# Two-layer encoder trunk on one core: how the last two heads' outputs, the reload of the other mixture chunks and the first W_out products are ordered

## What is computed

```python
attn = latent_attention(q_nope, q_rope, k_nope, k_rope, v)      # 8 heads, 64 wide
conv = gate_b * short_conv(gate_c * conv_in, w_conv[i])         # 512 channels
mix = jnp.concatenate([group_rms_norm(attn, g_attn_out[i], N_HEADS),
                       group_rms_norm(conv, g_conv_out[i], CONV_GROUPS)], axis=-1)
x = x + rms_norm(mix @ w_out[i], g_post_mix[i])
```

## Time and profile before

| what | value |
|---|---|
| time, median of 3 runs | 2876.78 us (2875.25 to 2877.29) |
| time of the profiled execution | 2878.98 us |
| its span, first to last instruction | 2877.2 us |
| mean granted TensorE clock | 0.992 of full |
| busy: TensorE, weight load, VectorE, ScalarE | 97%, 80%, 60%, 42% |
| end of attention in layer 0 and layer 1 | about 515 to 562 us, 1927 to 1973 us |

### The profile page before, as it was taken

How to read it: one execution, slowest core, us unless ns; L and a number is a source line. 1 busy time by engine, 2 the same in 40 slices (tenths; PEclk the granted TensorE clock), 3 DMA queues, 4 the chain that set the end, 5 groups by cost and what they waited for, 6 DMA issues and landing times.

```text
span 2877.2 us, 34913 instructions
## 1 busy us (share of the span) xinstructions
PE 2799.8 (97%) x13184; PEld 2311.0 (80%) x13184; DVE 1717.7 (60%) x2300; ACT 1203.0 (42%) x1917; POOL 113.9 (4%) x105
## 2 busy tenths in 40 slices
PE   6999999899999999999999999998999999999996
PEld 5878888688888888888887788887888888888885
DVE  4367888356544444458765588872844444444786
ACT  4336777454211211226643377773621121121473
POOL 0221000000000000000012200000000000000000
PEclk9999999999999999999999999999999999999998
DMA  4121110621111111112332111134211111111232
GB/s 149 59 74 47 32 32 23 221 91 59 51 38 57 44 44 58 44 66 96 103 108 73 56 38 32 27 106 163 82 54 40 58 44 44 58 44 44 73 103 73
DMA packets 64587, 194.93 MB, mean 68 GB/s; under 512 B 8288, under 2 KB 8288, under 8 KB 64480
## 3 DMA queue, kind: packets, MB, share of 16 engines
q1 hardware_dynamic: 64480, 193.49, 20.1%
HBM read 168.22 MB, written 25.23 MB: 67 GB/s over the span
## 4 chain that ended last, share of the span: by engine, by line
PE 93%; ACT 2%; DVE 2%; DMA 1%; issue 1%; SPq 0%; ACTq 0%; DVEq 0%
PE ps L821 28%; PE ps L823 28%; PE ps L822 28%; PE ps L988 3%; PE ps L1013 2%; PE ps L1012 2%; PE ps L1022 1%; DMA mix_lo<-yl 1%; PE ps L867 0%; PE ps L889 0%; PE ps L860 0%; ACT pth L1246 0%; DMA raw<-w_units 0%; ACT pr L1426 0%; ACT hh L1246 0%
## 5 line engine op out<-in xcount | busy, mean ns | idle before, releaser
L821 PE MATMUL ps<-hh,wh 128*128 128x512 f32 x2192 | 872.1, 398 | 25.1 <-DVE wl L1633 23.8
L823 PE MATMUL ps<-hh,wl 128*128 128x512 f32 x2192 | 856.0, 391 | 0.0
L822 PE MATMUL ps<-hl,wh 128*128 128x512 f32 x2192 | 855.9, 390 | 0.0
L821 PEld LDWEIGHTS ps<-hh,wh 128*128 128x128 f32 x2192 | 413.6, 189 | 119.7 <-issue 28.4
L822 PEld LDWEIGHTS ps<-hl,wh 128*128 128x128 f32 x2192 | 413.5, 189 | 93.5 <-issue 8.7
L823 PEld LDWEIGHTS ps<-hh,wl 128*128 128x128 f32 x2192 | 413.0, 188 | 86.7
L1246 ACT ACTIVATE wh<-raw 128x1024 fp32r<-128x1024 f32 x244 | 254.7, 1055 | 390.3 <-PE ps L823 369.8
L821 PE MATMUL ps<-gh,wh 128*128 128x512 f32 x1024 | 398.6, 389 | 0.0
L823 PE MATMUL ps<-gh,wl 128*128 128x512 f32 x1024 | 398.4, 389 | 0.0
L822 PE MATMUL ps<-gl,wh 128*128 128x512 f32 x1024 | 398.3, 389 | 0.0
L1976 DVE TENSOR_TENSOR xf<-xf,ps 128x512 f32<-128x512 f32 x464 | 310.9, 684 | 146.0 <-PE ps L823 145.5
(11 more groups left out here) (137 smaller groups left out, 3028.9 us busy)
## 6 DMA issues: line engine op xcount, KB each, us to landing
raw<-w_units SPq DMA_DIRECT2D x240, 512.0 KB, 3.3
hh<-mix_hi SPq DMA_DIRECT2D x16, 512.0 KB, 6.6
hl<-mix_lo SPq DMA_DIRECT2D x16, 512.0 KB, 7.3
stage<-w_head SPq DMA_DIRECT2D x16, 320.0 KB, 2.9
xf<-x_in SPq DMA_DIRECT2D x4, 1024.0 KB, 8.9
mix_hi<-cyh SPq DMA_DIRECT2D x8, 512.0 KB, 2.6
mix_lo<-cyl SPq DMA_DIRECT2D x8, 512.0 KB, 3.7
sq<-sums SPq DMA_DIRECT2D x32, 128.0 KB, 2.8
```

The lines of the kernel that those rows point to most:

```text
L821: nc.tensor.matmul(dst, ah, bh, start=start, stop=False)
L822: nc.tensor.matmul(dst, ah, bl, start=False, stop=False)
L823: return nc.tensor.matmul(dst, al, bh, start=False, stop=stop)
```

## The change

Heads 6 and 7 write the high and low part of their normalised output directly into chunk 3 of `hh`/`hl` (`high_at`, `low_at`); their stores to DRAM and the reload of chunk 3 are gone. Chunks 4, 7, 0, 1, 2 are loaded in SyncE's block of head 6 instead of head 7. The splits of W_out's units 0 to 3 are spread: unit 0 in head 6, units 1, 2, 3 in head 7. On TensorE, parts of outputs 0 and 1 stand between the last head's steps, and `var.1` of head 7 between the parts of output 2. The diff, cut to what the steps need:

```diff
-MIX_STORED = 16 * 2 * (CONV // P + 2 * HEADS)
+MIX_STORED = 16 * 2 * (CONV // P + 2 * (HEADS - 2))
...
 ATT_PE = steps("""
...
-q.1.0 turn.0.4.1 pv.0.1.0 pv.0.1.1 score.0.7 turn.0.5.0 turn.0.5.1 q.1.1 turn.0.6.0 turn.0.6.1 score.1.0
-pv.0.2.0 turn.0.7.0 turn.0.7.1 var.0.0 score.1.1 pv.0.2.1
+q.1.0 turn.0.4.1 pv.0.1.0 pv.0.1.1 score.0.7 turn.0.5.0 turn.0.5.1 mix.0.0 q.1.1 turn.0.6.0 turn.0.6.1 mix.0.1
+score.1.0 pv.0.2.0 turn.0.7.0 turn.0.7.1 var.0.0 mix.1.0 score.1.1 pv.0.2.1
...
 ATT_ACT = steps("""
-high.0.0.0 high.0.0.1 exp.0.1 y.-1.0 k.1.0 v.1.0 exp.0.2 high.0.1.0 high.0.1.1 exp.0.3 k.1.1 v.1.1 out.-1.1
-high.0.2.0 high.0.2.1 square.-1.1 high.0.3.0 high.0.3.1 unit.0 ln.-1.1 exp.0.4 v_turned.1 high.0.4.0 r.-1.1
-exp.0.5 high.0.4.1 q.1.0 exp.0.6 y.-1.1 high.0.5.0 high.0.5.1 last.0 out.0.0 exp.0.7 high.0.6.0 q.1.1
-high.0.6.1 last.1 square.0.0 high.0.7.0 high.0.7.1 exp.1.0 ln.0.0 r.0.0 last.2 last.3
+high.0.0.0 high.0.0.1 exp.0.1 y.-1.0 k.1.0 v.1.0 last.7.1 exp.0.2 high.0.1.0 high.0.1.1 exp.0.3 k.1.1 v.1.1 out.-1.1
+high.0.2.0 high.0.2.1 square.-1.1 high.0.3.0 high.0.3.1 unit.0 last.6.0 last.7.2
+ln.-1.1 exp.0.4 v_turned.1 high.0.4.0 r.-1.1 exp.0.5 high.0.4.1 q.1.0 last.7.3 exp.0.6 y.-1.1 high.0.5.0
+high.0.5.1 out.0.0 exp.0.7 high.0.6.0 q.1.1 high.0.6.1 square.0.0 high.0.7.0 high.0.7.1 exp.1.0 ln.0.0 r.0.0
...
 ATT_DVE = steps("""
+scale.-1.0 low.0.0.0 least.0.2 low.0.0.1 k.1.0 last.7.1 least.0.3 low.0.1.0 low.0.1.1 y.-1.0 k.1.1 sum.-1.1 low.0.2.0
+low.0.2.1 least.0.4 low.0.3.0 low.0.3.1 den.0.0 least.0.5 v_turned.1 least.0.6 unit.0 last.6.0
+last.7.2 q.1.0 scale.-1.1 low.0.4.0 low.0.4.1 last.7.3 q_low.1.0 least.0.7 low.0.5.0 low.0.5.1 q.1.1 sum.0.0
+low.0.6.0 low.0.6.1 den.0.1 least.1.0 q_low.1.1 low.0.7.0 low.0.7.1 y.-1.1 least.1.1
...
         if kind == "last":
+            if h == ahead:
+                yield (kind, h, *more)
+        elif kind == "mix":
             if h == HEADS - 1:
-                yield kind, h, ahead
+                yield (kind, h, ahead, *more)
...
+        def high_at(h, a, t):
+            return yh[rows(a), :] if h < HEADS - 2 else hh[rows(a), PAIRS - 1, hs(t)]
...
                 for h in range(HEADS):
-                    if h:
+                    if 0 < h < HEADS - 1:
                         store_attention((h - 1) // 2, (h - 1) % 2, 0)
...
-                sp.wait_ge(q_out, (L + 1) * 2 * HEADS)
-                sp.wait_ge(mix_stored, L * MIX_STORED + MIX_STORED - 96)
-                for c in (4, 7, 0, 1, 2):
-                    load_mix(c, mix_in)
-                store_sums(HEADS - 1, 1)
-                store_attention(PAIRS - 1, 0, 1)
-                load_sums(HEADS - 1, 1)
-                for w in range(O_AT + RAW, O_AT + SLOTS):
-                    load(L, w)
+                    if h == HEADS - 2:
+                        load(L, O_AT + RAW)
+                        sp.wait_ge(q_out, (L + 1) * 2 * HEADS)
+                        sp.wait_ge(mix_stored, (L + 1) * MIX_STORED)
+                        for c in (4, 7, 0, 1, 2):
+                            load_mix(c, mix_in)
+                        load(L, O_AT + RAW + 1)
+
                 sp.wait_ge(s_out, (L + 1) * HEADS * STEPS)
                 for c in (5, 6):
                     load_mix(c, mix_56)
+                store_sums(HEADS - 1, 1)
+                load_sums(HEADS - 1, 1)
                 load(L, O_AT + SLOTS)
-                store_attention(PAIRS - 1, 1, 0)
-                store_attention(PAIRS - 1, 1, 1)
-                sp.wait_ge(mix_stored, (L + 1) * MIX_STORED)
-                load_mix(3, mix_last)
...
+                def mix_first(n, piece):
+                    if piece == 0:
+                        unit_ready(L, O_AT + n)
+                        pe.wait_ge(mix_in, (L + 1) * 160)
+                        pe.wait_ge(s_exp, step(L, HEADS - 1, 6 + n // 2) + 1)
+                        mix_part(n, (4, 7), True, False)
+                    else:
+                        mix_part(n, (0, 1, 2), False, False)
...
+                mix_first(1, 1)
+                mix_first(2, 0)
+                variances(HEADS - 1, 1, 1)
+                mix_first(2, 1)
+                mix_first(3, 0)
+                mix_first(3, 1)
                 pe.wait_ge(mix_56, (L + 1) * 64)
                 for n in range(4):
                     mix_part(n, (5, 6), False, False)
-                pe.wait_ge(mix_last, (L + 1) * 32)
-                for n in range(4):
+                    if n == 0:
+                        pe.wait_ge(o_lo, (L + 1) * 2 * HEADS + 1)
                     mix_part(n, (3,), False, True).then_inc(mix_out, 1)
...
-                    act.wait_ge(mix_stored, L * MIX_STORED + 128 + (h * 2 + t) * 32)
-                    copy(yh[rows(a), :], of[rows(a), :]).then_inc(o_hi, 1)
+                    if h < HEADS - 2:
+                        act.wait_ge(mix_stored, L * MIX_STORED + 128 + (h * 2 + t) * 32)
+                    copy(high_at(h, a, t), of[rows(a), :]).then_inc(o_hi, 1)
```

More of the change, by code:

```diff
@@ L534, in encoder @@
         mix_56 = sem("mix_56")
-        mix_last = sem("mix_last")
         mix_out = sem("mix_out")
@@ L617, in rows, with low_at @@
             return slice(a * V_DIM, (a + 1) * V_DIM)
+        def high_at(h, a, t):
+            return yh[rows(a), :] if h < HEADS - 2 else hh[rows(a), PAIRS - 1, hs(t)]
+        def low_at(h, a, t):
+            return yl[rows(a), :] if h < HEADS - 2 else hl[rows(a), PAIRS - 1, hs(t)]
         def gate_of(n):
@@ L754, in load_sums, with load_mix @@
                     sp.dma_start(sq[rows(1 - h % 2), 0, :], sums[O:O + 1].partition_broadcast(V_DIM)).then_inc(den_in, 16)
+                def load_mix(c, done):
+                    sp.dma_start(hh[:, c, :].bitcast(f32), mix_hi[c]).then_inc(done, 16)
+                    sp.dma_start(hl[:, c, :].bitcast(f32), mix_lo[c]).then_inc(done, 16)
                 load_head(2)
                 for h in range(HEADS):
-                    if h:
+                    if 0 < h < HEADS - 1:
                         store_attention((h - 1) // 2, (h - 1) % 2, 0)
@@ L768, in _ @@
                             store_attention((h - 1) // 2, (h - 1) % 2, 1)
-                def load_mix(c, done):
-                    sp.dma_start(hh[:, c, :].bitcast(f32), mix_hi[c]).then_inc(done, 16)
-                    sp.dma_start(hl[:, c, :].bitcast(f32), mix_lo[c]).then_inc(done, 16)
-                sp.wait_ge(q_out, (L + 1) * 2 * HEADS)
-                sp.wait_ge(mix_stored, L * MIX_STORED + MIX_STORED - 96)
-                for c in (4, 7, 0, 1, 2):
-                    load_mix(c, mix_in)
-                store_sums(HEADS - 1, 1)
-                store_attention(PAIRS - 1, 0, 1)
-                load_sums(HEADS - 1, 1)
-                for w in range(O_AT + RAW, O_AT + SLOTS):
-                    load(L, w)
+                    if h == HEADS - 2:
[5 more added lines that the diff above has]
+                        load(L, O_AT + RAW + 1)
                 sp.wait_ge(s_out, (L + 1) * HEADS * STEPS)
@@ L1022, in variances, with mix_part @@
                     nc.tensor.matmul(ps[:, 6 + t, :], cst[:, 3 + a, :], sq[:, 0, :], start=True, stop=True).then_inc(o_var, 1)
+                def mix_part(n, order, start, stop):
+                    m, t = OUT_OUTS[n]
+                    slot = slot_of(OUT_UNIT[n])
+                    for i, k in enumerate(order):
+                        last = split_product(ps[:, n % 4, :], wh[:, slot, k, :], wl[:, slot, k, :],
+                                             hh[:, k, hs(t)], hl[:, k, hs(t)], start and i == 0, stop and i == len(order) - 1)
+                    return last
+                def mix_first(n, piece):
[6 more added lines that the diff above has]
+                        mix_part(n, (0, 1, 2), False, False)
                 def attend(h):
@@ L1052, in attend @@
                             values(o, a, *n)
+                        elif kind == "mix":
+                            mix_first(*n)
                         elif kind == "var" and (o, n[0]) != (HEADS - 1, 1):
@@ L1877, in low_of_output @@
                     dve.wait_ge(o_hi, (L * HEADS + h) * 2 + t + 1)
-                    low(yl[rows(a), :], of[rows(a), :], yh[rows(a), :]).then_inc(o_lo, 1)
+                    low(low_at(h, a, t), of[rows(a), :], high_at(h, a, t)).then_inc(o_lo, 1)
                 def attend(h):
```

## The result

The changed kernel takes 2852.64 us (median of 4 runs, 2850.86 to 2857.15) against 2877.03 us (2875.25 to 2877.38) before: ratio 0.9914, 95% interval 0.9902 to 0.9927, a gain of 24.4 us. Forecast was 2850.8 with a range of 2845.5 to 2861.

The account below looks back on a forecast made before the run. TensorE, 97% busy, bounds the kernel, so only its 31.9 us of non-work can go; less 5.9 us of new waits and handovers, 26 us gained. From 2878.98 to 2853.0, median 2.2 lower: 2850.8 us, range 2845.5 to 2861.

Parts of the forecast that it names:

- The stretch: TensorE from head 7's step 5 transposes to output 4's first matmul: 46.34 and 45.36 us, 29.9 us of it work per layer.
- 31.9 us of non-work: Stretch time that is not work, 16.4 us in layer 0 and 15.5 in layer 1; the most reordering can gain.
- unit 3: W_out load issued at 504.5 behind 5.2 MB, landing at 516.3 (516.8 in layer 1); its split on ScalarE waits for it.
- Early splits: Splits of units 1 and 2 early in head 7 delay TensorE's step 5 transposes by 0.8 us, bounds 0 to 2.3.
- Wait of the first part: TensorE's first mixture part waits for `exp.6`, queued behind unit 3's split: 1.0 us in layer 0, 1.5 in layer 1.
- Transposes of step 6: In head 7 they wait another 0.7 us because `high.5`, `least.7` and `low.5` end late.
- The recorded 32.4 and 33: Forecast us from step 5's transposes to output 4's first matmul, in layers 0 and 1.
- The covers named for the second variance and chunk 3: Head 7's square ready 1.4 us before its second variance; chunk 3 ready at 539, wanted at 541: both cost 0.
- (a): Unit 3 comes late, TensorE idles in one piece, clock falls: worst 8 us less gain per layer, likely 5, 2861; 13%.
- (b): Low clock without a longer wait; one short and one long low stretch give 2857.6 us; 12%.
- (c): First mixture part holds up head 7 if loads land 13 us late; 26 us lost, or slower at 2883; 3%.
- (d): No change: a later stage, the residual or unit loads, gives the gain back, 2876.8 us; 3%.

Follow-up runs that it names:

- splits_late: Changed kernel with unit 2's split behind head 7's square on ScalarE and unit 3's split behind head 7's first y: 2846.92 us, ratio to before 0.9891.
- splits_only: Kernel before with only the new split lists and the loads of units 2 and 3 moved up, ahead of the mixture loads: 2860.40 us, ratio 0.9939.
- unit3_ahead: Changed kernel with unit 3's load issued after chunks 4, 7, 0 and ahead of chunks 1, 2: 2851.03 us.
- the changed kernel again: Changed kernel without any edit, run once more to see its spread: 2852.47 us (5 runs, 2851.47 to 2853.60).
- via_dram: Changed kernel with heads 6 and 7 again written to DRAM and chunk 3 loaded back, its products last for all four outputs: 2855.94 us.
- no_fill: Changed kernel with the three mixture parts taken from between the last head's steps and put behind the head: 2857.99 us.
- loads_late: Changed kernel with the ten mixture loads started in head 7 again, units 2 and 3 loaded ahead of them: 2872.67 us, ratio to before 0.9982.

## Why the prediction held

*What bounds.* The stretch, its 29.9 us of work and its 31.9 us of non-work were right: splits_late comes within about 0.7 us of that floor in each layer, and no run went below it.

*Which part pays.* The chain of the earlier trace rows named the splits as the block ahead of head 7's output, and splits_only alone gains 16.4 of 24.8 us. The rest needs the earlier loads, the fill and the direct write together: without fill 5.4 us are lost, without the direct write 3.3, and with the fill but without the early loads 20. These losses do not add up to the rest, because each part leans on the others.

*Transfers.* Mixture loads issued near 499 and landed before they were asked for; unit 3 was taken to land at 516.3 and released its split at 517.07, but this run is 0.7 us later already at the anchor (493.17 against 492.51), so it was right within 0.1 us. The Trainium skill states (DMA: Bandwidth & Descriptors, Queues, rings and completion order) that on each DMA engine descriptors are consumed in ring order. These rows agree (12.5 us behind ten loads), and so does unit3_ahead, where ScalarE no longer waited.

*The terms of the sum.* Early splits: the transposes of step 5 start 24.1 us behind the anchor instead of 23.2, 0.9 us, forecast 0.8 (24.1 instead of 23.4, 0.7 us, in layer 1). Wait of the first part 0.87 and 2.07 us, forecast 1.0 and 1.5. Transposes of step 6: 0.27 us as the profile counts it, forecast 0.7. Non-work in all 56.1 - 53.1 = 3.0 us in layer 0, forecast 2.7, and 57.3 - 53.3 = 4.0 us in layer 1, forecast 3.2 (53.3, because the kernel before reached step 5 in 23.4 us there). The miss is layer 1: I carried the late landing of head 5's store over, but not that SyncE's issues take longer there. It issued unit 3 at 1903.06, 12.7 us behind the anchor, against 11.4 us in layer 0. The term also varies: in the changed kernel again the first part waited 1.10 and 1.64 us. From the transposes of step 5 to output 4 the two layers take 32.0 and 33.2 us. The recorded 32.4 and 33 count the 0.8 us of the early splits, which lie ahead of these transposes; without it, and with the 0.2 us of handovers, they would be 31.8 and 32.3, so that 33 comes so near to 33.2 is in part luck.

*Off in size.* The stores of heads 6 and 7 were priced at 0; via_dram shows about 3 us: 1.6 us by a wait of 0.4 and 0.9 us on ScalarE that no longer has a cover, 0.7 us by the reload, the rest open. The covers named for the second variance and chunk 3 held.

*Rivals.* (a) and (b), the low clock, did not occur in this stretch in the two profiled executions of the changed kernel, but did in splits_only and no_fill, so they were near. (c) needed 13 us of later landing; loads_late made 9.7 us of wait and takes 0.2% less than the kernel before. (d): no later stage gave anything back.

## What to carry to other kernels

Look at what stands ahead of a stage's last chain in its engines' queues: a split that waits for a load holds everybody behind it, and moving the splits and their loads was worth two thirds of this change. Here a load issued behind 5 MB on one queue arrived 12.5 us after its issue and not 3.3, so place the instructions that need it by that, on every engine that touches it. Work put between the steps of a stage paid here mostly by keeping TensorE from standing in one piece, but its own operands must be there early, because the whole stage stands behind it.

## What the runs showed of the hardware

The granted clock fell behind short stands of TensorE: to 0.50 (1.2 GHz) behind a wait of 2.2 us in both layers of splits_only, and in no_fill within a wait of 3.0 us in layer 0 and behind one of 2.5 us in layer 1. With waits of 1.1 and 1.5 us the kernel before had a low stretch in layer 1 and none in layer 0, and the changed kernel had none with 0.87 or 2.07 us. The low stretches measured from 3.2 to 13.6 us, and more than half of the loss of no_fill was theirs. So a wait of 2 to 3 us on TensorE cost, in these runs, that wait and up to 2.7 us more. Four stores of 0.5 KB behind 5 MB on the same queue took 6.1 us from their issue to the issue of the load that waits for them, where they had taken 2.1 us.
